# Second projection: query and key chunks computed transposed, weights stationary; next scores beside a value product

## The reference, cut to what matters

```python
h = rms_norm(x, g_pre[l])
proj = h @ w_in[l]                       # 256 x 2048 times 2048 x (11280 + 4 * 2048)
(a_val, a_gate, sq, sk, sv, s_gate, cq, ck, cv, c_gate, c_lr,
 mq, m_gate, g_logits) = jnp.split(proj, split_at, axis=-1)
y_a = pool_mixer(a_val, a_gate, w_pool[l], pool_scale[l])
y_b = swa_mixer(sq, sk, sv, s_gate)      # 3 groups of 4 heads of 128: banded softmax attention
y_c = gla_mixer(cq, ck, cv, c_lr, c_gate, ...)   # 4 heads: linear attention with decays
y_m = mem_attn(mq, m_gate, mem, g_mem[l], w_mem_kv[l])   # 4 heads over 256 memory tokens
```

## Time and profile before

| | |
|---|---|
| median of 3 runs | 3416.32 us (3415.52 to 3417.68) |
| profiled execution, its own time | 3416.22 us |
| its span, first to last instruction | 3414.4 us |
| second projection in the span | about 2278 to 2827 us |
| TensorE busy, matmuls, whole span | 2910.7 us (85%), 11296 instructions |
| weight loads | 2049.1 us (60%), 11296 |
| VectorE busy | 1839.0 us (54%) |
| ScalarE busy | 1141.7 us (33%) |
| GpSimd busy | 2340.6 us (69%) |

### The profile page before, as it was taken

How to read it: one execution, slowest core, us unless ns; L and a number is a source line. 1 busy time by engine, 2 the same in 40 slices (tenths; PEclk the granted TensorE clock), 3 DMA queues, 4 the chain that set the end, 5 groups by cost and what they waited for, 6 DMA issues and landing times. The chain is left out here.

```text
span 3414.4 us, 30933 instructions
## 1 busy us (share of the span) xinstructions
PE 2910.7 (85%) x11296; PEld 2049.1 (60%) x11296; DVE 1839.0 (54%) x2409; ACT 1141.7 (33%) x1837; POOL 2340.6 (69%) x1120
## 2 busy tenths in 40 slices
PE   6999999999977666665656766589999999999998
PEld 2787888888853333322222322248888888888887
DVE  3577536413588787778988887751157322111122
ACT  3322455444421111111221111134455444444443
POOL 0244676488667575757776577858767688888887
PEclk9999999999988888867678897789999999999999
DMA  9899844365699999999999999985545456656554
GB/s 401 329 348 341 306 161 155 114 222 185 240 415 426 426 426 425 427 427 427 420 427 427 426 421 427 427 326 187 173 153 182 136 188 199 223 192 208 188 190 167
DMA packets 307900, 1014.82 MB, mean 297 GB/s; under 512 B 21900, under 2 KB 26600, under 8 KB 241056
## 3 DMA queue, kind: packets, MB, share of 16 engines
q1 hardware_dynamic: 231320, 475.62, 40.2%
q0 software_dynamic: 73728, 536.90, 37.3%
q10 hardware_dynamic: 2700, 0.32, 0.1%
HBM read 1008.54 MB, written 4.23 MB: 297 GB/s over the span
## 5 line engine op out<-in xcount | busy, mean ns | idle before, releaser
L732 POOL TENSOR_TENSOR block_weights_lo<-weight_ring,block_weights_hi 128x1024 fp32r<-128x1024 f32 x596 | 1441.9, 2428 | 596.0 <-ACT block_weights_hi L725 581.3
L1923 PE MATMUL banks<-up_rows,pick_diagonal 128*128 128x512 f32 x1024 | 674.8, 820 | 447.1 <-DMA up_rows<-peer_up,picked_experts 389.2
L725 ACT ACTIVATE block_weights_hi<-weight_ring 128x1024 fp32r<-128x1024 f32 x608 | 641.0, 1059 | 972.8 <-PE banks L3073 316.1
L1923 PEld LDWEIGHTS banks<-up_rows,pick_diagonal 128*128 128x128 f32 x1024 | 260.4, 267 | 829.2 <-issue 733.2
L1780 POOL DMA_INDIRECT up_rows<-peer_up,picked_experts x256 | 487.0, 1903 | 332.2 <-PE banks L1923 97.5
L2286 DVE CUSTOM_DVE_ANT_0 down_rows<-down_rows,h_tokens 128x2048 f32<-128x2048 f32 x256 | 583.9, 2291 | 189.6 <-DMA down_rows<-peer_down,picked_experts 186.3
L1772 POOL DMA_INDIRECT down_rows<-peer_down,picked_experts x256 | 405.8, 1585 | 103.0 <-issue 77.4
L2233 DVE SCALAR_TENSOR_TENSOR expert_sum<-up_rows,pick_share,expert_sum 128x2048 f32<-128x2048 f32 x125 | 293.9, 2351 | 49.8 <-ACT pick_share L2067 45.8
L2061 ACT ACTIVATE pick_gelu<-pick_dots 128x2 f32<-128x2 f32 x127 | 25.8, 203 | 843.4 <-DVE pick_dots L2286 843.4
L2504 PE MATMUL banks<-block_weights_hi,h_T_hi 128*128 128x512 f32 x688 | 275.4, 400 | 0.8 <-POOL block_weights_lo L732 0.8
L2506 PE MATMUL banks<-block_weights_hi,h_T_lo 128*128 128x512 f32 x688 | 268.5, 390 | 0.0
(11 more groups left out here) (555 smaller groups left out, 4386.1 us busy)
## 6 DMA issues: line engine op xcount, KB each, us to landing
weight_ring<-w_in SPq DMA_DIRECT2D x232, 1024.0 KB, 4.9
cond_ring<-w_ada SPq DMA_DIRECT2D x128, 512.0 KB, 6.3
weight_ring<-w_ada SPq DMA_DIRECT2D x32, 1024.0 KB, 8.3
weight_ring<-w_out SPq DMA_DIRECT2D x32, 1024.0 KB, 4.9
weight_ring<-peer_query SPq DMA_DIRECT2D x12, 1024.0 KB, 16.8
weight_ring<-w_ret_out SPq DMA_DIRECT2D x8, 1024.0 KB, 4.9
weight_ring<-w_mlstm_out SPq DMA_DIRECT2D x8, 1024.0 KB, 4.8
weight_ring<-w_mem_kv SPq DMA_DIRECT2D x8, 1024.0 KB, 11.3
```

Of the source, the lines that this page charges most:

```text
L725: act.activation(self.hi[:, self.place(slot, h)], ring.tile[:, slot, h * self.HALF:(h + 1) * self.HALF], ACT.Copy).then_inc(self.hi_ready, 1)
L732: pool.tensor_tensor(self.lo[:, at], ring.tile[:, slot, h * self.HALF:(h + 1) * self.HALF], self.hi[:, at], ALU.subtract).then_inc(ring.us ...
L1923: mm = pe.matmul(ps[:, 4 + b], diag[:, G % 2], up[:, p % ROWS, b * CG:(b + 1) * CG], start=(G % PER_TB == 0), stop=(G % PER_TB == PER_TB - ...
```

## The change

Nine chunks (three of queries and three of keys of the banded heads, the memory queries, and `CQ` and `CK` of the linear attention) are computed by a new function `dense_turned`. It keeps 128 x 128 of the weights stationary and moves the 256 tokens, so each block of 128 columns comes out with its columns on the partitions and tokens along them: already transposed. Each such chunk takes 192 matmuls of 256 columns where it took 96 of 512. The scale is put into the copy out of PSUM. `turn_qk`, `copy_qk` and `gla_turn` are gone, and the queries and keys are read where they lie (`own`); the memory keys, which another phase computes, are turned once at slots 8 and 9 (`turn_keys`). In each group of chunks the order is value, query, key. `scores` of head n stays at slot H+1; `weigh` of head n moves from slot H+3 to H+4, which is where the next head's scores are, and `weigh` and `scores` swap their PSUM roles: the value product now goes to bank X, so that it stands beside scores in bank Y. The three products of a linear-attention head read their query and key from `p2`. Two of the gate multiplications are regrouped (`gated_heads`).

```diff
-SECOND_CHUNKS = tuple(first + g * CG for g in range(3) for first in (SQ, SK, SV)) + (
+SECOND_CHUNKS = tuple(first + g * CG for g in range(3) for first in (SV, SQ, SK)) + (
...
+        QUERIES = tuple(SQ + g * CG for g in range(3)) + (MEMQ,)
+        TURNED = QUERIES + tuple(SK + g * CG for g in range(3)) + (CQ, CK)
+        own = lambda first, h: p2[:, h % 4 // 2, first + h % 2 * T:first + (h % 2 + 1) * T]
+        own_blocks = lambda first, h: own(first, h).rearrange("p (b n) -> p b n", b=TB)
...
                 if c == LSE_AT // SLOTS + 1:
                     sp.wait_ge(o_done, NSWA)
-                    sp.wait_ge(qk_turned, NSWA)
...
+            def dense_turned(m):
+                c, t = divmod(m, SLOTS)
+                for h in range(2):
...
+                    for kk in range(split.HALF):
+                        k = t * TILE_K + h * split.HALF + kk
+                        hi, lo = e.hT_hi[:, k], e.hT_lo[:, :, k]
+                        for j in range(4):
...
+                            out, cols = ps[:, 2 * (c % 2) + j // 2, j % 2 * T:(j % 2 + 1) * T], slice(j * P, (j + 1) * P)
+                            w_hi, w_lo = split.hi[:, at, kk, cols], split.lo[:, at, kk, cols]
+                            pe.matmul(out, w_hi, hi, start=(k == 0 and j % 2 == 0), stop=False, skip_group_check=True)
+                            pe.matmul(out, w_hi, lo, start=False, stop=False, skip_group_check=True)
+                            mm = pe.matmul(out, w_lo, hi, start=False, stop=(k == KB - 1), skip_group_check=True)
+                    mm.then_inc(split.free, 1)
...
             def weigh(n):
                 pe.wait_ge(ex_out, n + 1)
-                pe.wait_ge(sc_ready, n + 1)
...
-            def turn_qk(n):
-                pe.wait_ge(cols_out, (head_chunk(n) + 1) * TB)
...
             for m in range(SLOTS_ALL):
+                for i in range(2):
+                    if m == KEYS_AT + i:
+                        turn_keys(i)
                 for n in range(NH):
-                    if m == HEAD_AT[n] + 3:
+                    if m == HEAD_AT[n] + 4:
                         weigh(n)
                 for n in range(NH):
-                    if m == HEAD_AT[n]:
-                        turn_qk(n)
                     if m == HEAD_AT[n] + 1:
                         scores(n)
...
-                    if m == GLA_AT[h]:
-                        gla_turn(h)
...
-                if m >= EARLY:
+                if CHUNKS[m // SLOTS] in TURNED:
+                    dense_turned(m)
+                elif m >= EARLY:
                     dense(m)
...
-            def copy_qk(n):
...
+            def gated_heads(c, y):
+                dve.wait_ge(gate_out, (c - GATE0 + 1) * TB)
+                by_block = p2[:, :, y:y + CG].rearrange("p a (b t n) -> p t a b n", b=2, t=TB)
+                for tb in range(TB):
+                    gate = p2[:, tb, CHUNKS[c]:CHUNKS[c] + CG].rearrange("p (a b n) -> p a b n", a=2, b=2)
+                    step(dve.tensor_tensor(gate, gate, by_block[:, tb], ALU.mult))
...
                     if m == GLA_AT[h]:
-                        dve.wait_ge(gla_turned, h + 1)
+                        dve.wait_ge(cols_out, (written(CK) + 1) * TB)
                         dve.wait_ge(exps, 3 * H)
-                        q, k = ps[:, V, 0:T], ps[:, V, T:2 * T]
+                        q, k = own(CQ, h), own(CK, h)
```

More of the change, by code:

```diff
@@ L2507, in dense, with turn_keys @@
                     mm.then_inc(split.free, 1)
+            def dense_turned(m):
+                c, t = divmod(m, SLOTS)
+                for h in range(2):
+                    at = split.place(t, h)
+                    if h == 0:
+                        pe.wait_ge(split.first_ready, m + 1)
+                    else:
+                        pe.wait_ge(ring.used, (base + c) * SLOTS + t + 1)
+                    for kk in range(split.HALF):
+                        k = t * TILE_K + h * split.HALF + kk
+                        hi, lo = e.hT_hi[:, k], e.hT_lo[:, :, k]
+                        for j in range(4):
+                            if k == 0 and j % 2 == 0 and c >= 2:
+                                pe.wait_ge(cols_out, (c - 2) * TB + j // 2 + 1)
+                            out, cols = ps[:, 2 * (c % 2) + j // 2, j % 2 * T:(j % 2 + 1) * T], slice(j * P, (j + 1) * P)
[4 more added lines that the diff above has]
+                    mm.then_inc(split.free, 1)
+            def turn_keys(i):
+                if i >= 1:
+                    pe.wait_ge(keys_out, i)
+                for h in (2 * i, 2 * i + 1):
+                    for b in range(TB):
+                        tr = pe.transpose(ps[:, X, h % 2 * T + b * P:h % 2 * T + (b + 1) * P], mem_key(h, b), e.ident[:])
+                tr.then_inc(keys_turned, 1)
             def weigh(n):
                 pe.wait_ge(ex_out, n + 1)
-                pe.wait_ge(sc_ready, n + 1)
                 for tb in range(TB):
@@ L2514, in weigh, with scores @@
                     for i, b in enumerate(keys):
-                        mm = pe.matmul(ps[:, Y, tb * P:(tb + 1) * P], exT[:, b, tb * P:(tb + 1) * P], value(n, b), start=(i == 0), stop=(i == len(keys) - 1))
+                        mm = pe.matmul(ps[:, X, tb * P:(tb + 1) * P], exT[:, b, tb * P:(tb + 1) * P], value(n, b), start=(i == 0), stop=(i == len(keys) - 1))
                 mm.then_inc(o_done, 1)
-            def turn_qk(n):
+            def scores(n):
                 pe.wait_ge(cols_out, (head_chunk(n) + 1) * TB)
+                if n == NSWA:
+                    pe.wait_ge(keys_out, 2)
                 if n >= 1:
-                    pe.wait_ge(ex_out, n)
-                for b in range(TB):
-                    pe.transpose(ps[:, X, b * P:(b + 1) * P], p2[:, b, q_at(n):q_at(n) + P], e.ident[:])
-                for b in range(TB):
-                    tr = pe.transpose(ps[:, X, T + b * P:T + (b + 1) * P], key(n, b), e.ident[:])
-                tr.then_inc(qk_turned, 1)
-            def scores(n):
-                pe.wait_ge(qk_out, n + 1)
-                if n >= 1:
-                    pe.wait_ge(o_out, n)
+                    pe.wait_ge(sc_ready, n)
                 for tb in range(TB):
                     reach = (tb + 1) * P if n < NSWA else T
-                    mm = pe.matmul(ps[:, Y, tb * T:tb * T + reach], qk[:, tb * P:(tb + 1) * P], qk[:, T:T + reach], start=True, stop=True)
+                    mm = pe.matmul(ps[:, Y, tb * T:tb * T + reach], q_T(n)[:, tb * P:(tb + 1) * P], k_T(n)[:, 0:reach], start=True, stop=True)
                 mm.then_inc(s_done, 1)
@@ L2558, in decay_logits @@
                 pe.matmul(ps[:, V, 0:T], w_alpha[:, h * P:(h + 1) * P], e.lrT[:], start=True, stop=True).then_inc(z_done, 1)
-            def gla_turn(h):
-                pe.wait_ge(cols_out, (written(CK) + 1) * TB)
-                pe.wait_ge(neg_abs, H)
-                if h >= 1:
-                    pe.wait_ge(state_ready, (NC - 1) * h)
-                for a, first in enumerate((CQ, CK)):
-                    for tb in range(TB):
-                        tr = pe.transpose(ps[:, V, a * T + tb * P:a * T + (tb + 1) * P], p2[:, tb, first + h * P:first + (h + 1) * P], e.ident[:])
-                tr.then_inc(gla_turned, 1)
             def gla_scores(h):
@@ L2703, in _ @@
                     gate_columns(m // SLOTS - 1)
+                for i in range(2):
+                    if m == KEYS_AT + i:
+                        copy_keys(i)
                 for n in range(NH):
-                    if m == HEAD_AT[n] + 3:
+                    if m == HEAD_AT[n] + 4:
                         copy_out(n)
                 for n in range(NH):
-                    if m == HEAD_AT[n]:
-                        copy_qk(n)
                     if m == HEAD_AT[n] + 1:
@@ L2812, in combine @@
                 dve.wait_ge(o_out, NSWA)
-                o = [p2[:, tb, q_at(g * PER + h):q_at(g * PER + h) + P] for g in range(NG)]
+                o = [att_out(g * PER + h)[:, tb] for g in range(NG)]
                 step(dve.tensor_scalar(o[0], o[0], wt[:, h, tb:tb + 1], None, ALU.mult))
```

52 lines of the change are left out of this document (30 added, 22 removed).

## The result

The changed kernel takes 3431.21 us (median of 5 runs, 3430.72 to 3434.35), the one before 3416.32 us on the same chip: a ratio of 1.0045 with a 95% interval of 1.0034 to 1.0056. It is slower by 14.9 us, where I had predicted 3417.2 us and a range up to 3427. The profiled execution took 3432.35 us, its span is 3430.6 us (before 3414.4), with 12088 matmuls (11296 - 72 transposes + 864).

The account below looks back on a forecast made before the run. TensorE's own instruction order was taken to bound the second projection. 3416.2 - 8.0 (transposes) + 0.8 (turned matmuls) + 7.7 (VectorE's lock) + 0.5 (weight-piece slack) = 3417.2 us; range 3408 to 3427.

Parts of the forecast that it names:

- The turned matmuls: Nine chunks, 1728 matmuls of 256 columns: 0.45 ns more each, 0.8 us, between bounds of 113.7 and 188 ns a matmul.
- one pair: Two 128-column weight loads, at 2544.81 and 2544.92 us, read as showing that loads overlap, just under the 114 ns wanted.
- The comparison with the low-rank product: 256-column matmuls in the trace of before, 46 steps of 113.9 ns, but with 16 weight columns.
- the weight loads set the pace: Rival, turned chunks: loads decide from 118.3 ns a matmul; at 128 ns 24.7 us, total 3433 us; chance 0.06.
- The transposes: TensorE's queue in the second projection: 80 removed, eight of memory keys added, net 72 at 111 ns, 8.0 us less.
- The lock of VectorE behind GpSimd: Linear-attention products with two SBUF inputs stand until GpSimd's subtraction ends: 7.7 us more, between 0 and 18.8.
- The wait of 0.9 us: TensorE's wait two slots after head 0's products, expected to go as VectorE catches up; subtracted from the 5.6 us stall.
- Three times in a row: VectorE's eight-column operation was said to wait thus behind GpSimd, as support for the rival that every head pays, chance 0.14.
- The slack of the weight pieces: Heads 8 to 11, where ScalarE holds weight pieces behind the decay chain: 0 to 2 us more, taken 0.5.
- The rule that I gave little weight: Skill page's issue gap, about 81 ns for 128 columns and 131 for 512: cutting 864 matmuls would add 56 us.

Follow-up runs that it names:

- the run without stalls: Changed kernel with the three linear-attention products two slots earlier and VectorE's clip of the scores ahead of the group weights: 3418.43 us, ratio 1.0002 to the kernel before.
- the second profile: Changed kernel run again, unaltered, on the same chip as the repeated run with superfluous matmuls in the waits: phase 563.6 us, median 3432.79 us, ratio 1.0045.

## Why the prediction was wrong, point by point

- **The turned matmuls: the step that failed.** The prediction took "a value near the lower end", 0.45 ns for each, 0.8 us in all. It is 6.3 ns and 10.9 us. I had read the load's pace from one pair, 0.11 us apart, "just under the 114 ns wanted", and taken a load that is shorter than the stream as hidden. The run with 128 moving columns goes at 112 ns, so the pair was no accident; but under 256 columns the pace is 120 and not 114. A load pace just under that of the stream was no reason to take the loads as hidden. Why the two don't overlap fully stays open. The comparison with the low-rank product could not show that: its loads have 16 columns. Nearest was the rival "the weight loads set the pace", which decides from 118.3 ns and had a chance of 0.06; the runs bear it out in so far as the pace depends on the width of the block.
- **The transposes**, -8.0 us: right as far as the sums show. In the run without stalls -8.0 + 10.9 - 0.9 gives 550.6 us and 550.1 was measured.
- **The lock of VectorE behind GpSimd**: right in kind and place. Head 0: a stall of 5.6 us predicted (4.7 after the 0.9 that goes), 5.0 measured. Head 2: 2.5 taken within 0.3 to 5.0, 4.4 measured; the copy of four decays met a subtraction as well, which I had not counted. Head 1: 0.5 and 0; head 3: 0 and 0. The wait of 0.9 us went, as said. Together 8.4 net against 7.7. ("Three times in a row", said of the eight-column operation, was twice: 2.3, 2.3 and 0.17 us.) The Trainium skill's rule ("SBUF — State Buffer", section "SBUF: two separate sides") of an exclusive lock for a whole instruction fits every row of the products: they last 0.42 us or to the end of a subtraction, nothing between, and with an operand in PSUM always 0.42.
- **The clock after the waits**: the second step that failed, for it isn't in the sum at all. Half clock sets in before each wait of 4.4 to 5 us is over and lasts 6.8 us (3.4 behind one wait of the second profile), 4.8 us of loss in the two. A stall costs more than its own length. That there is such a price could have been read in the trace of before. In an earlier phase TensorE waits for DMA again and again, here for 5.0 and for 2.3 us, and both times works at half clock behind it (timeline of TensorE, then busy time by stretch; TensorE is less busy there between its waits, so the rows give a price but no limit for this phase):

```profile
1128.52 1.19 PE L1923 MATMUL banks<-up_rows,pick_diagonal 128*128 128x512 f32 x1 [5.01 <-DMA up_rows<-peer_up,picked_experts]
...
1399.68 2.34 PE L1923 MATMUL banks<-up_rows,pick_diagonal 128*128 128x512 f32 x3 [2.26 <-DMA up_rows<-peer_up,picked_experts]
```

```profile
1128.00:1134.00 6.00, 5.48 (x7) 2.40 (x8) 2.30 (x2) 0.00 (x0) 2.32 (x3) 0.50 1.03 426
...
1400.20:1403.60 3.40, 3.40 (x6) 1.32 (x5) 2.65 (x2) 0.00 (x0) 3.10 (x2) 0.51 1.01 426
```

- **The slack of the weight pieces**, +0.5: TensorE waits 0.8 us for them, as before. The term is 0.
- **The rule that I gave little weight**: the Trainium skill ("TensorE: Matmul & The Clock Gate", Back-to-back issue gap) would have given +56 us for cutting the matmuls, by an estimate of 98 ns for 256 columns that lies a third of the way from 128 to 512, not halfway. The page's figures don't hold here (227.5 ns for 512 columns, 120 for 256), but that shorter matmuls keep a worse pace per column, as they say, does, at 10.9 us.

With the pace alone mended the sum would have been 3427.3 us; with the clock too, 3432.1, against 3432.35 us of the profiled execution. That closeness is in part luck: the waits were put 0.7 us too low and the slack 0.5 too high.

## What to carry to other kernels

Turning a product round trades transposes for shorter matmuls with as many full weight loads each. Where full loads alone keep about the pace of the stream behind them (112 and 114 ns here), don't take them as hidden (120 ns was measured), and multiply the few ns by the count before calling the trade free: a turned chunk lost 1.2 us here to save 0.9. When work moves from PSUM to SBUF on VectorE, look for what GpSimd does at that moment, and at what stands behind the work in VectorE's queue, since one wait hides the next. And price a stall of TensorE with the slow clock behind it, from stalls that the trace already has.

## What the runs showed of the hardware

- In this phase waits of TensorE of 4.4 and 5.0 us went with 3.4 or 6.8 us at a granted clock of 0.50, beginning before the wait was over; waits of up to 2.4 us did not, but in an earlier phase one of 2.3 us did. Putting 3.9 us of superfluous matmuls into each wait kept the clock at 1.00 and made the kernel 3.7 us faster.
- The clock also fell with hardly any idleness: for about 24 us amid matmuls of 128 moving columns at 112 ns, right behind a wait of 0.8 us. With 256 columns at 120 ns and no such wait, in the run without stalls, it did not. Which of the two differences matters isn't shown.
- Stationary blocks of 128, 96 and 64 columns under 256 moving columns give a mean of 119.9, 116.1 and 115.2 ns a matmul, that of 64 as a mixture of some 113.5 and 120.0; 128 under 128 gives 111.7.
- Beside a GpSimd subtraction, VectorE's products of 256 columns with both inputs in SBUF, additions of 8 and a copy of 4 lasted until the subtraction was over (up to 2.7 us). Products with one operand in PSUM took 0.42 us there, as without it.
